# Asking for u rows a round ahead of v rows, in a written-out GpSimd program

## The reference

```python
s1, s2 = scores of the two query halves against 128 sub-keys each     # per token and head
v1, i1 = top_k(s1, 16);  v2, i2 = top_k(s2, 16)
cs, ci = top_k(all 256 sums v1 + v2, 16)
experts = i1[ci // 16] * 128 + i2[ci % 16]      # 8 heads * 16 = 128 experts per token
gates   = softmax(cs)
z   = einsum('td,ted->te', xn, u[experts])      # a dot with each expert's u row
act = gelu(z) * gates
out = einsum('te,ted->td', act, v[experts])     # the weighted sum of the v rows
h   = h + out
```

## Time and profile before

| | |
|---|---|
| three timed runs | 1772.48, 1776.9, 1778.13 us |
| median | 1776.9 us |
| profiled execution, span from first to last instruction | 1768.2 us, 18597 instructions |
| the page's time for that execution beside its span | none is given |
| busy: PE, VectorE, GpSimd, ScalarE | 1434.2, 1116.1, 1143.6, 276.3 us |
| HBM traffic | 649.13 MB, mean 367 GB/s |
| indirect requests | 512 for u, 512 for v, median 7.2 and 7.1 us from issue to landing |
| PE, gathering (line 1240) | 972.8 us busy, 267.5 idle before it |
| VectorE, dots (line 748) | 613.0 us busy, 260.0 idle before them |
| GpSimd, copies of indices (line 361) | 23.4 us for 64 |

### The profile page before, as it was taken

The page is one execution under the profiler, slowest core; times in us unless marked ns, Lnnn a source line. Parts: engine busy times, 40 slices in busy tenths (PEclk is TensorE's granted clock), DMA queues, the critical chain, the costliest instruction groups (busy, mean ns, idle before and its releaser), DMA issues.

```text
span 1768.2 us, 18597 instructions
## 1 busy us (share of the span) xinstructions
PE 1434.2 (81%) x5144; PEld 835.4 (47%) x5144; DVE 1116.1 (63%) x2843; ACT 276.3 (16%) x757; POOL 1143.6 (65%) x1094
## 2 busy tenths in 40 slices
PE   7968797999898596988899778889789766776776
PEld 6867454655664253544357334454346422332332
DVE  2648786777463868475566578665567499444454
ACT  1211111211111111121111110122111101111111
POOL 0004777677657777767776676667775767777775
PEclk9989898999999898989899889899999987988889
DMA  8855999999999999999999999999999989999998
GB/s 321 307 217 178 352 414 410 410 411 410 413 399 411 341 370 392 377 381 384 374 413 412 386 322 413 358 408 374 372 397 411 339 317 326 354 358 369 368 389 327
DMA packets 164520, 649.13 MB, mean 367 GB/s; under 512 B 18656, under 2 KB 18912, under 8 KB 151648
## 3 DMA queue, kind: packets, MB, share of 16 engines
q0 software_dynamic: 147456, 536.94, 79.6%
q1 hardware_dynamic: 16992, 111.27, 15.8%
HBM read 647.09 MB, written 1.05 MB: 367 GB/s over the span
## 4 chain that ended last, share of the span: by engine, by line
PE 57%; DVE 21%; DMA 7%; issue 6%; POOL 5%; ACT 4%; POOLq 0%; DVEq 0%; ACTq 0%; SPq 0%; PEldq 0%
PE acc L1240 35%; PE bank L1061 9%; DVE u_ring L748 9%; PE bank L1057 8%; DMA u_ring<-in_u,idx_cur 6%; POOL v_ring L370 3%; POOL u_ring L370 2%; DVE xn L385 1%; ACT diag L988 1%; DVE arena L385 1%; ACT xT L825 1%; PE bank L1195 1%; DVE ef L692 1%; DMA v_ring<-in_v,idx_cur 1%; ACT arena L840 1%
## 5 line engine op out<-in xcount | busy, mean ns | idle before, releaser
L1240 PE MATMUL acc<-v_ring,diag 128*128 128x512 f32 x2040 | 972.8, 638 | 267.5 <-ACT diag L988 266.0
L1240 PEld LDWEIGHTS acc<-v_ring,diag 128*128 128x128 f32 x2040 | 413.2, 205 | 805.5 <-issue 569.1
L748 DVE SCALAR_TENSOR_TENSOR u_ring<-u_ring,xp 128x1024 f32<-128x1024 f32 x512 | 613.0, 1225 | 260.0 <-DMA u_ring<-in_u,idx_cur 250.0
L370 POOL DMA_INDIRECT v_ring<-in_v,idx_cur x512 | 578.5, 1130 | 270.4 <-PE acc L1240 135.5
L370 POOL DMA_INDIRECT u_ring<-in_u,idx_cur x512 | 539.7, 1054 | 195.0 <-issue 132.0
L1061 PE MATMUL bank<-w_ring,xT 128*128 128x256 f32 x768 | 171.9, 384 | 7.3 <-ACTq L826 7.3
L1061 PEld LDWEIGHTS bank<-w_ring,xT 128*128 128x128 f32 x768 | 146.6, 192 | 30.5 <-ACTq L826 8.9
L988 ACT ACTIVATE diag<-ident,act_w 128x128 f32<-128x128 f32 x510 | 156.2, 388 | 17.7 <-DVE act_w L762 15.9
L1057 PE MATMUL bank<-xT,w_ring 128*128 128x128 f32 x1280 | 148.4, 279 | 6.2 <-ACTq L826 6.2
L1057 PEld LDWEIGHTS bank<-xT,w_ring 128*128 128x128 f32 x1280 | 147.4, 195 | 11.4 <-ACTq L826 7.6
L762 DVE SCALAR_TENSOR_TENSOR act_w<-ez,gz 128x8 f32<-128x8 f32 x64 | 10.9, 170 | 197.1 <-ACT ez L983 197.1
(11 more groups left out here) (128 smaller groups left out, 794.6 us busy)
## 6 DMA issues: line engine op xcount, KB each, us to landing
w_ring<-in_wall SPq DMA_DIRECT2D x92, 1024.0 KB, 8.5
u_ring<-in_u,idx_cur POOLq DMA_INDIRECT x512, 7.2
v_ring<-in_v,idx_cur POOLq DMA_INDIRECT x512, 7.1
u_ring<-in_wall SPq DMA_DIRECT2D x4, 1024.0 KB, 9.7
v_ring<-in_wall SPq DMA_DIRECT2D x4, 1024.0 KB, 9.8
gains<-in_gains SPq DMA_DIRECT2D x5, 512.0 KB, 13.4
h<-in_x SPq DMA_DIRECT2D x2, 512.0 KB, 9.1
arena<-in_amask SPq DMA_DIRECT2D x1, 576.0 KB, 10.3
```

The source lines that it names most:

```text
L370: nc.gpsimd.indirect_dma_start(out=ring[:, r, :], out_offset=None, in_=table, in_offset=bass.IndirectOffsetOnAxis(ap=idx_cur[:, g * RING + ...
L748: V.scalar_tensor_tensor(out=u_ring[:, r, :], in0=u_ring[:, r, :], scalar=1.0, in1=xp[:, t, :], op0=ALU.mult, op1=ALU.mult, accum_out=z[:, ...
L1240: ins = M(acc[:, s], diag[:, r, :], v_ring[:, r, s], start=False, stop=hi == ROUNDS and n == hi - lo - 1 and r == count_of - 1)
```

## The change

`idx_cur`, its copy and two semaphores (`pool_tick`, `idx_set`) are gone. The loop over heads is replaced by a program written out for all 64 rounds, so that each request reads its index column of `idx_all` at a fixed address and each wait is for a constant. The order of requests was u(n), v(n), u(n+1), v(n+1). It is now u(0), u(1), v(0), u(2), v(1), u(3) and so on: the u rows of the next round ahead of the v rows of this one. Rings, counts, and what VectorE, ScalarE, PE and SyncE do are as before.

```diff
-        idx_cur = sb("idx_cur", [P, TOPK], U32)
...
-        pool_tick = sem("pool_tick")
...
-        idx_set = sem("idx_set")
...
-            with pool.Fori(0, PHASES * HEADS) as i:
-                pool.wait_ge(idx_ready, i + 1)
-                for g in range(GROUPS):
-
-                    pool.wait_ge(v_used, i * TOPK + (g * RING + 1))
-                    nc.gpsimd.tensor_copy(idx_cur[:, g * RING:(g + 1) * RING],
-                                          idx_all[:, bass.ds(i * TOPK + g * RING, RING)]).then_inc(idx_set, 1)
-                    pool.wait_ge(idx_set, i * GROUPS + (g + 1))
-                    for ring, table, arrived, used, credit in ((u_ring, u_d, u_in, u_used, 0),
-                                                               (v_ring, v_d, v_in, v_used, 1)):
-                        for r in range(RING):
-
-                            pool.wait_ge(used, i * TOPK + (g * RING + r + 1 + credit))
-                            pool.sem_inc(pool_tick, 1)
-                            nc.gpsimd.indirect_dma_start(
-                                out=ring[:, r, :], out_offset=None, in_=table,
-                                in_offset=bass.IndirectOffsetOnAxis(ap=idx_cur[:, g * RING + r:g * RING + r + 1], axis=0))\
-                                .then_inc(arrived[r], 16)
+            def fetch(ring, table, arrived, used, credit, n, r):
+
+                slot = n * RING + r
+                pool.wait_ge(used, slot + 1 + credit)
+                nc.gpsimd.indirect_dma_start(
+                    out=ring[:, r, :], out_offset=None, in_=table,
+                    in_offset=bass.IndirectOffsetOnAxis(ap=idx_all[:, slot:slot + 1], axis=0)).then_inc(arrived[r], 16)
+
+            def fetch_u(n):
+                if n % GROUPS == 0:
+                    pool.wait_ge(idx_ready, n // GROUPS + 1)
+                for r in range(RING):
+                    fetch(u_ring, u_d, u_in, u_used, 0, n, r)
+
+            def fetch_v(n):
+                for r in range(RING):
+                    fetch(v_ring, v_d, v_in, v_used, 1, n, r)
+
+            fetch_u(0)
+            for n in range(PHASES * ROUNDS):
+                if n + 1 < PHASES * ROUNDS:
+                    fetch_u(n + 1)
+                fetch_v(n)
```

## The result

The kernel after the change takes 1935.27 us (median of 4 runs, 1926.9 to 1944.12) against 1777.52 us before (4 runs, 1772.48 to 1779.26): the ratio is 1.0908 with an interval of 1.0864 to 1.0952. Slower was forecast, but at 1834 us and 1850 at most; the profiled span grew by 156.9 us instead of 57. In the profile after, the lines have moved: the dots are line 750, the requests 357, the weights `act_w` 764, the tanh 985, the diagonals 990, PE's gather 1242.

What follows compares the result with a forecast made beforehand. A loop through PE bounds phases 0 to 2, GpSimd's requests most of phase 3. The terms 20 + 19 + 20 - 2 = +57 on 1768.2 give 1825, with 8.7 around it 1834 us (0.60; range 1812 to 1850, for all 1788 to 1850).

Steps and rivals of the forecast that it cites:

- the eleven: Rounds 1, 3, 4, 17, 19, 20, 23, 33, 35, 36, 39: routing or side work before dots; only these priced.
- Rival A: GpSimd keeps pace with the dots, so v lands at D + 16.2, 5.3 behind PE's old start: 1796 us; chance 0.19.
- B: Rival: the delay stops at PE, still in side work at D + 21; about 1750 us, chance 0.12.
- C: Rival: it evens out, late v fetched while PE catches up; within 5 us of no change, 1777; chance 0.05.
- D: Rival: long program's fetching adds 10, no recovery 22: 1865 us, 0.04. In times, D is a round's dots' start.
- The step that failed: Phase 0 after round 4: PE nearly without gaps keeps its 20 us lateness; about 2 come back, 2 are lost again.
- the loop that the prediction itself had described: Phases 0 to 2: PE's gather, side work, ScalarE's tanh, VectorE's weights, next dots; a late gather delays the next dots.
- The winning back of 11 us: Phase 1 after round 23: PE, busy 94.3 of 109 us, wins back 11 of 14.7, leaving +19; phase 2 likewise.
- The chains for the eleven rounds: Phases 0 to 2: v lands at D + 21.0, PE starts 10.1 later where dots come late; +20, +19, +20.
- Phase 3: GpSimd-bound stretch: 5 us lost at its start, 9.5 saved without the copy, 3 at the end; about -2.
- The tail: At the end PE gathers 14 rows after v(62) lands, in place of 6 behind the last dots: about +3.
- The contention: GpSimd requests beside two-input VectorE dots take 1.97 us instead of 0.94; without it the delay of 10.1 would be 5.4.

Runs made afterwards that it cites:

- experiment 5: Against the kernel after: old order u(n), v(n) except in rounds 1, 3, 4, 17, 19, 20, 23, 33, 35, 36, 39, which keep the new order; 1827.2 us.
- experiment 1: Against the kernel after: written out with fixed addresses and no copy, but in the old order u(n), v(n); 1736.7 us, 0.9796 of the kernel before.
- experiment 6: Against the kernel after: new order only in the other 37 rounds of phases 0 to 2, old order elsewhere; 1893.67 us, 1.0682 of the kernel before.
- 11: Against the kernel after: old order throughout, new order in round 10 alone; 1746.07 us, 0.9858 of the kernel before.
- experiments 8 to 10: Against the kernel after: old order, plus the index copy (1741.98 us), plus an increment of `pool_tick` between wait and request (1736.58 us), plus both (1768.77 us).
- Experiment 7: Against the kernel after: each dot replaced by a plain sum over the u row, with one SBUF input; 1852.3 us, 1.0448 of the kernel before.

## Why the prediction was wrong

**The bound and the mechanism: right.** The v requests stand behind the eighth dot of their own round: they come at D + 15.3 in round 17 and D + 16.4 in round 20 (15.3 was forecast) and PE starts at D + 21.6 and D + 22.5 (21.0 was). The releaser is as forecast. The idle time near 20 us isn't there: it is 11.12 in round 17. That follows from the failed step below, since round 16 is late too and PE reaches the wait later; in experiment 5, where only the eleven are late, PE's timeline has it in round 17:

```profile
644.45 15.60 PE L1246 MATMUL acc<-v_ring,diag 128*128 128x512 f32 x32 [19.93 <-DMA v_ring<-in_v,idx_all]
```

GpSimd waits 312.8 us for u slots. The gap between requests stayed at 0.30, and the written-out program, which experiment 1 has too, costs nothing that shows. Rival A is out by the v requests' time, B by the dots of round 19 (659.61 before, 725.83 after), C by the phases; D would have put its cost in every written-out kernel.

**The step that failed** is the one by which only eleven rounds were priced: "Afterwards PE works nearly without a gap and keeps it". It took a busy PE for one that a late v can't reach. But a PE without gaps that comes to its gather at D + 12 has no more room than one that has waited for it: the v rows are there at D + 21 all the same, and the next dots hang on the gather by the loop that the prediction itself had described. What had to be read was PE's start against D, round by round, and not the idle time before it. By it the prediction's own D + 21.0 gives 36 rounds with a shortfall, 258 us in all. Experiments 5, 6 and 11 show this: the other rounds cost 157 us, and a single one of them 9.5. Of the 107 us that phases 0 to 2 came out above the forecast (166 against 59), this is the larger part: the kernel after, which has the new order in the other rounds too, is 39.6, 32.7 and 23.4 us longer in these phases than experiment 5, 96 in all. The shortfall tells which rounds can lose, and not exactly what: rounds 0, 16 and 32 give theirs back (experiment 6), and neighbours overlap.

**The winning back of 11 us** in rounds 24 to 28 didn't happen. The prediction named GpSimd as the limit there and still let PE catch up, though a late GpSimd can't. In experiment 5, which has the old order in those rounds, PE was 53.6 us later than in experiment 1 at round 23 and 55.8 at round 28; against the kernel before it comes back by 4.6, but that is the shorter period of the written-out program, which gives experiment 1 6.8 there. In the kernel after it went from +89.5 to +99.6 against before: its dots stand beside v requests and make half of them 1.88 to 1.99 us, as in GpSimd's timeline of the requests for v(24), beside round 25's dots:

```profile
889.18 1.88 POOL L357 DMA_INDIRECT v_ring<-in_v,idx_all  x1 [0.30 <-issue]
...
895.95 1.99 POOL L357 DMA_INDIRECT v_ring<-in_v,idx_all  x1 [0.30 <-PE acc L1242]
```

**The chains for the eleven rounds** were otherwise nearly right. By the starts of the gathers in the kernel after and before, round 1 was put 10 late and was 9.4; round 4 20 and was 19.8. Round 3 was put 16 late and was 23: its v rows, beside the weight stream, took 12 us to land (asked for at 263.1, there at 275.0) and not 5.7. In experiment 5 the phases lose 20.1, 32.5 and 31.8, against 20, 30 and 30 without the win-back.

**Phase 3: right in sum, by two wrong terms.** With its tail it came out at -7.5, inside the bounds of -8 and +8. The period is 20.44 us, under the 21 to 21.5 forecast: the 1.7 us of longer requests, which the prediction kept, nearly went with the copy (experiments 8 to 10). That made 21.1 instead of 4.5 net. (The prediction's rows give 0.73 us for the copy, 0.20 + 0.83 - 0.30, and it took 0.9; that is 2 us over these rounds.) The tail was put at 3 and took 13.6. That the two errors met inside the bounds is luck. Both last gathers are there at once, 56 matmul records in 27.1 us from D(63) + 10.3, where before one gather was left at D(63) + 11.8. The row is PE's last gather:

```profile
1893.73 27.13 PE L1242 MATMUL acc<-v_ring,diag 128*128 128x512 f32 x56 [3.68 <-DMA v_ring<-in_v,idx_all]
```

**The contention** was counted at its right size. The Trainium skill ("GPSIMD Engine Reference", 8. Key points) says that GpSimd contends with VectorE instructions that have two SBUF inputs. Experiment 7 agrees, with 0.94 us beside the one-input sums and up to 1.99 beside the two-input dots, and makes it worth some 82 us of the kernel after.

## What to carry to other kernels

When a request on an in-order queue is put ahead of another, it brings its own wait along: ask what the later one now waits for, and give its landing as a time after that event, for every round. The room that a round has is the consumer's old start less the new landing, both counted from that event, and not the idle time before the consumer: one that is busy without a gap and starts early has none to give. Then ask what the next round waited for, since a delay that nothing waits for is given back. And an improvement in one edit (here 35 us by writing out) is found only when the other edit is undone: written out in the old order, the kernel takes 1736.7 us and beats both.

## What the runs showed of the hardware

- An indirect request of 128 rows takes 0.94 us on GpSimd, the same beside a one-input VectorE sum of 1.21 us and beside a product of 0.96 us whose second input is in PSUM, and up to 1.97 to 1.99 beside back-to-back operations of 1.22 us with two SBUF inputs.
- A request behind a copy on the same engine starts 0.27 us after it when it carries its wait itself and 0.83 when an increment stands between wait and request; requests that lie beside dots are then also longer, by some 0.1 us on the average of all. Together, and only together, they cost 32 us of 1769.
- In the kernel after the first v row of a round lands 6 to 8 us after its request in three rounds of four, and after 12 to 17 beside the weight stream (rounds 3 and 22).
